# Head 0's queries in two token halves, ScalarE evicts the queries, and low parts behind a norm's first steps

## The reference, cut to what matters

```python
q = (zc @ peer_wq).reshape(128, 8, 2, 128)          # zc: 128 tokens, normalised
s1 = einsum('chd,hkd->chk', q[:, :, 0], k1)          # 128 keys per head and half
s2 = einsum('chd,hkd->chk', q[:, :, 1], k2)
v1, i1 = top_k(s1, 16); v2, i2 = top_k(s2, 16)
top_s, top_pos = top_k(v1[..., :, None] + v2[..., None, :], 16)   # of 256 candidates
gate = softmax(top_s)
act = gelu(einsum('chkd,cd->chk', peer_u[expert], zc))
out = einsum('chk,chkd->cd', gate * act, peer_v[expert])
```

## Time and profile before

| | us |
|---|---|
| median of three runs (2816.95 to 2819.15) | 2817.71 |
| the profiled execution, its own time | 2813.53 |
| its span in the profile | 2811.6 |
| TensorE busy | 2384.8 (85%) |
| VectorE busy | 1748.5 (62%) |
| ScalarE busy | 782.2 (28%) |
| GpSimd busy | 520.3 (19%) |

### The profile page before, as it was taken

One profiled execution on the slowest core, in us unless ns is written; L12 is line 12 of the kernel. 1 busy time (PEld: TensorE's weight loads), 2 busy tenths in 40 slices (PEclk: granted clock), 3 DMA queues, 4 the chain that ended last, 5 costly groups with the idle time before them and its releaser, 6 DMA issues.

```text
span 2811.6 us, 29260 instructions
## 1 busy us (share of the span) xinstructions
PE 2384.8 (85%) x10874; PEld 1692.4 (60%) x10874; DVE 1748.5 (62%) x2554; ACT 782.2 (28%) x1151; POOL 520.3 (19%) x594
## 2 busy tenths in 40 slices
PE   8998899999999999899899857777777777777776
PEld 8986677888888888799788722222222222222222
DVE  6975547665666566677656995555655555555444
ACT  5423555443444344545430101001010110111010
POOL 0000000000000000100012453333333333333341
PEclk9998899999999999999999989999999999999999
DMA  7643254556555655544588999999999999999997
GB/s 223 185 99 119 74 168 148 190 183 194 181 193 180 193 180 168 176 150 150 164 255 305 421 420 422 422 421 421 422 421 421 422 421 422 421 421 421 421 422 326
DMA packets 339901, 798.92 MB, mean 284 GB/s; under 512 B 23313, under 2 KB 270699, under 8 KB 273771
## 3 DMA queue, kind: packets, MB, share of 16 engines
q0 software_dynamic: 73728, 536.90, 45.9%
q1 hardware_dynamic: 266091, 260.96, 29.3%
HBM read 795.72 MB, written 2.10 MB: 284 GB/s over the span
## 4 chain that ended last, share of the span: by engine, by line
DMA 37%; PE 13%; DVE 7%; issue 1%; POOL 1%; ACT 1%; DVEq 0%; POOLq 0%; PEldq 0%; ACTq 0%
DMA row<-in_peer_v,expert 30%; DMA row<-in_peer_u,expert 6%; DVE row L2145 4%; PE pl L798 3%; PE pl L1143 3%; PE pl L805 3%; PE pl L1082 1%; PE pl L801 1%; PE pl L802 1%; POOL row L709 1%; DVE wlo L1649 1%; DMA raw<-in_w_out 0%; ACT whi L1170 0%; DVE sq_r L2165 0%; DVE l_xc L2031 0%
## 5 line engine op out<-in xcount | busy, mean ns | idle before, releaser
L1143 PE MATMUL pl<-row,diag 128*128 128x512 f32 x1856 | 860.1, 607 | 332.3 <-DMA row<-in_peer_v,expert 327.2
L2145 DVE CUSTOM_DVE_ANT_0 row<-row,pg 128x2048 f32<-128x2048 f32 x256 | 581.6, 2286 | 444.9 <-DMA row<-in_peer_u,expert 443.5
L1143 PEld LDWEIGHTS pl<-row,diag 128*128 128x128 f32 x1856 | 337.7, 191 | 854.7 <-issue 456.5
L1649 DVE TENSOR_TENSOR wlo<-raw,whi 128x1024 fp32r<-128x1024 f32 (+1 forms) x436 | 517.1, 1207 | 378.3 <-ACT whi L1170 375.9
L1170 ACT ACTIVATE whi<-raw 128x1024 fp32r<-128x1024 f32 (+1 forms) x436 | 443.6, 1039 | 420.9 <-PE pl L805 401.7
L798 PE MATMUL pl<-x_split,whi 128*128 128x512 f32 x1888 | 477.6, 395 | 13.0 <-DVE x_split L1657 7.5
L798 PEld LDWEIGHTS pl<-x_split,whi 128*128 128x128 f32 x1888 | 341.5, 190 | 76.5 <-issue 9.2
L805 PE MATMUL pl<-x_split,wlo 128*128 128x256 f32 x2656 | 373.2, 284 | 6.1 <-DVE wlo L1649 6.1
L805 PEld LDWEIGHTS pl<-x_split,wlo 128*128 128x128 f32 x2656 | 358.6, 192 | 25.7 <-DVE wlo L1649 7.1
L709 POOL DMA_INDIRECT row<-in_peer_u,expert x256 | 240.7, 940 | 634.9 <-PE pl L1143 500.0
L1562 ACT ACTIVATE diag<-ident,dots 128x128 f32<-128x128 f32 x232 | 90.8, 399 | 887.4 <-PE pl L1143 861.0
(11 more groups left out here) (312 smaller groups left out, 1545.9 us busy)
## 6 DMA issues: line engine op xcount, KB each, us to landing
raw<-in_w_in SPq DMA_DIRECT2D x50, 1024.0 KB, 5.4
raw<-in_w_gate SPq DMA_DIRECT2D x44, 1024.0 KB, 5.1
raw<-in_w_up SPq DMA_DIRECT2D x44, 1024.0 KB, 5.1
raw<-in_w_out SPq DMA_DIRECT2D x32, 1024.0 KB, 5.5
raw<-in_w_down SPq DMA_DIRECT2D x32, 1024.0 KB, 5.4
wq<-in_peer_wq SPq DMA_DIRECT2D x16, 1024.0 KB, 11.2
raw<-in_w_down SPq DMA_DIRECT2D x16, 768.0 KB, 4.6
raw<-in_w_ukv SPq DMA_DIRECT2D x4, 1024.0 KB, 5.1
```

What stands on the lines that cost most here:

```text
L1143: last = mm(pl[q], diag[:, (at - 1) % 4, :], row[b][:, q * 512:(q + 1) * 512], start=(t == 1 and n == 0 and k == 0), stop=last_row, skip_g ...
L1649: V.tensor_tensor(wlo[:, n % 4, 0:k, :], w[:, :, f, :], whi[:, n % 4, 0:k, :].bitcast(F32), ALU.subtract)\
L2145: V.tensor_tensor_reduce(row[b][:], row[b][:], z_tok[:], 1.0, 0.0, ALU.mult, ALU.add, dots[:, at:at + 1])\
```

## The change

- Head 0's queries are made for the first 128 tokens (matmuls of 128 columns), its scores for them follow, and the second 128 tokens come behind all token-row transposes. `wq_used` 1 comes with the latter.
- ScalarE copies the queries out of PSUM, unscaled (`query_copy`), and the exponent of the gate is taken with the token's norm factor as its scale. `EVICT` and VectorE's `queries` go.
- The first block's choice is split: expert numbers 0 to 7 are worked out and released (`sel_first`) ahead of the second pass of the maximum, and 8 to 15 behind it. In block 0, `best_keys` for block 1 moves from product 3 to 8, `choose` from 6 to 10.
- The two tiles of a head's weights from head 1 on share a semaphore, and both halves wait for both tiles.
- In `residual`, the low weights of half 0 move from ahead of the norm to pass 2, those of half 1 from pass 3 to pass 4.

```diff
-        wq_in = [sem(f"wq_in{m}") for m in range(2 * PH)]
+        wq_in = [sem(f"wq_in0{m}") for m in range(2)]
+        wq_in += [s for s in [sem(f"wq_in{n}") for n in range(1, PH)] for _ in range(2)]
...
-                if table == "u" and k == 0:
+                if j == 0:
+                    pool.wait_ge(sel_first, 1)
+                elif (table == "u" and k == 0) or j == 8:
                     pool.wait_ge(sel_ready, t * PH + n + 1)
...
-                    pe.wait_ge(wq_in[2 * n + half], 16)
+                    pe.wait_ge(wq_in[2 * n + half], 32 if n else 16)
...
-            queries(0, (0,))
+            queries(0, (0,), (0,), q0_done)
             wide_total("n2")
-            queries(0, (1,))
-            peer_scores(0)
+            queries(0, (1,), (0,), q0_done)
+            peer_scores(0, (0,))
...
+            token_rows(0)
+            token_rows(1)
+            queries(0, tokens=(1,))
             queries(1)
             pe.wait_ge(tok_r, 8)
+            peer_scores(0, (1,))
             peer_scores(1)
...
+            def query_copy(n, tokens=range(TT), done=wq_used, ready=wq_ready):
+                act.wait_ge(done, 1 if done is q0_done else n + 1)
+                if n >= 2:
+
+                    act.wait_ge(sc_done, n)
+                c = slice(tokens[0] * P, (tokens[-1] + 1) * P)
+                copy(qh[:, n % 2, :, c], pl[n % 2].rearrange("p (f s) -> p f s", f=2)[:, :, c]).then_inc(ready, 1)
...
-                activation(g, g, ACT.Exp).then_inc(sel_exp, 1)
+                activation(g, g, ACT.Exp, scale=small[:, 56 + t:57 + t]).then_inc(sel_exp, 1)
...
-            for n in range(1, PH):
-                score_copy(n)
+            query_copy(0, (1,))
+            query_copy(1)
+            score_copy(0, (1,))
+            score_copy(1)
+            query_copy(2)
+            for n in range(3, PH):
+                query_copy(n)
+                score_copy(n - 1)
+            score_copy(PH - 1)
             gate_exp(0, 0)
...
-                weights_lo(unit, piece, halves=(0,))
                 dve.wait_ge(gained, 8 * turn)
...
-                    if k == 3:
-                        weights_lo(unit, piece, halves=(1,))
+                    if k in (2, 4):
+                        weights_lo(unit, piece, halves=(k // 2 - 1,))
...
-            queries(0)
...
-            choose(0, 0)
+            link(V.max(ctop[:, 0:8], cand[:]))
+            V.max_index(cpos[:, 0:8], ctop[:, 0:8], cand[:])
+            link(V.match_replace(cand2[:], ctop[:, 0:8], cand[:], NEG))
+            experts(0, 8, [work[:, m, :].rearrange("p (k j) -> p k j", k=8) for m in range(2)], sel_first)
+            link(V.max(ctop[:, 8:16], cand2[:]))
+            link(V.max_index(cpos[:, 8:16], ctop[:, 8:16], cand2[:]))
+            V.tensor_tensor(gate[:, 0:TOPK], ctop[:], ctop[:, 0:1].broadcast_to([P, TOPK]), ALU.subtract).then_inc(sel_max, 1)
+            experts(8, 16, [work[:, m, :].rearrange("p (k j) -> p k j", k=8) for m in range(2)], sel_ready)
...
-                    if (i, k) in EVICT:
-                        queries(EVICT[i, k])
```

More of the change, by code:

```diff
@@ L1069, in _, with queries @@
             pe.wait_ge(z_scaled, 8)
-            def queries(n, halves=(0, 1)):
-                bank = pl[n % 2]
+            def queries(n, halves=(0, 1), tokens=range(TT), done=wq_used):
+                bank, cols, width = pl[n % 2], tokens[0] * P, len(tokens) * P
                 for half in halves:
-                    if half == 0:
+                    if half == 0 and tokens[0] == 0:
                         pe.wait_ge(wq_ready, n + 1)
                     w = wq[2 * n + half]
-                    pe.wait_ge(wq_in[2 * n + half], 16)
+                    pe.wait_ge(wq_in[2 * n + half], 32 if n else 16)
@@ L1079, in queries @@
                     for t in range(KU):
                         for f in range(2):
-                            first = half == 0 and t == 0 and f == 0
-                            last = mm(bank[:, f * S:(f + 1) * S], w[:, t, f, :], mix[:, half * KU + t, :], start=first,
+                            first = half == 0 and t == 0 and f == 0 and tokens[0] == 0
+                            last = mm(bank[:, f * S + cols:f * S + cols + width], w[:, t, f, :],
+                                      mix[:, half * KU + t, cols:cols + width], start=first,
@@ L1083, in queries, with peer_scores @@
                                       stop=(half == 1 and t == KU - 1), skip_group_check=True)
                     if half == 1:
-                        last.then_inc(wq_used, 1)
-            def peer_scores(n):
-                pe.wait_ge(wq_ready, n + 3)
+                        last.then_inc(done, 1)
+            def peer_scores(n, tokens=range(TT)):
+                if n == 0 and tokens[0] == 0:
+                    pe.wait_ge(q0_ready, 1)
+                else:
+                    pe.wait_ge(wq_ready, n + 3)
@@ L1090, in peer_scores @@
                 if n >= 2:
                     pe.wait_ge(sc_ready, 2 * (n - 1))
[L1093 to L1096, removed]
-                last.then_inc(sc_done, 1)
-            queries(0, (0,))
+                for t in tokens:
+                    for half in range(2):
+                        m = 2 * t + half
+                        last = mm(pl[2 + n % 2][:, m * P:(m + 1) * P], qh[:, n % 2, half, t * P:(t + 1) * P],
+                                  keysT[:, half * PH + n, :], start=True, stop=True)
@@ new lines, in peer_scores, with token_rows @@
+                last.then_inc(sc_done, 1)
+            def token_rows(t):
+                pe.wait_ge(norm_inv, NI["n2"] + 1)
+                for m in range(4 * t, 4 * t + 4):
+                    f4 = m % 4
+                    if m == 4:
+                        pe.wait_ge(rstd_tok, 1)
+                    elif m == 5:
+                        pe.wait_ge(sc_ready, 1)
+                    elif m >= 6:
+                        pe.wait_ge(tok_r, m - 1)
+                    bank = pg[f4] if t == 0 else pl[3 - m % 2]
+                    for f in range(4):
+                        last = nc.tensor.transpose(bank[:, f * P:(f + 1) * P],
+                                                   res[:, f4 * 4 + f, t * P:(t + 1) * P], ident[:])
+                    last.then_inc(tok_T, 1)
@@ L2156, in sum_row @@
                     .then_inc(row_summed, 1)
[L2158 to L2166, removed]
             def row_weights(pair):
@@ L2192, in final_rows, with experts @@
                         .then_inc(fin_out, 1)
-            queries(0)
-            best_keys(0, 0)
-            choose(0, 0)
+            def experts(n_first, n_last, halves, done):
+                m = slice(n_first, n_last)
+                ci = cpos[:, m].bitcast(I32)
+                V.tensor_scalar(cposi[:, 0, m], ci, 4, None, ALU.logical_shift_right)
+                link(V.tensor_scalar(cposi[:, 1, m], ci, 15, None, ALU.bitwise_and))
+                link(V.tensor_copy(cposf[:, :, m], cposi[:, :, m]))
+                full = [P, n_last - n_first, TOPK]
+                for half in range(2):
+                    last = V.tensor_tensor(halves[half], wide(cposf[:, half, m], 2, full),
+                                           iota16[:].unsqueeze(1).broadcast_to(full), ALU.is_equal)
+                link(last)
+                for half in range(2):
+                    last = V.tensor_tensor(halves[half], halves[half], wide(top_f[:, half, :], 1, full), ALU.mult)
+                link(last)
+                for half in range(2):
+                    last = V.tensor_reduce(cposf[:, half, m], halves[half], AX.X, ALU.add)
+                link(last)
+                V.scalar_tensor_tensor(expert[:, m], cposf[:, 0, m], float(NKEY), cposf[:, 1, m], ALU.mult, ALU.add).then_inc(done, 1)
+            best_keys(0, 0)
+            link(V.max(ctop[:, 0:8], cand[:]))
[6 more added lines that the diff above has]
+            experts(8, 16, [work[:, m, :].rearrange("p (k j) -> p k j", k=8) for m in range(2)], sel_ready)
+            dve.wait_ge(sel_ready, 1)
             dve.wait_ge(rstd_tok, 1)
```

31 lines of the change are left out of this document (10 added, 21 removed).

## The result

The kernel after took 2837.08 us (median of 4 runs, 2829.93 to 2841.28), the kernel before 2818.43 us beside it: a ratio of 1.0058, 95% interval 1.0037 to 1.008, slower by 18.7 us. Predicted were 2836 us and +18. The profiled execution of after is the lowest of its four: 2829.93 us, span 2827.8, granted clock 0.973; before's was 2813.53 us. The profiles are thus 16.4 us apart. In five further executions after had 2835.6 us and a ratio of 1.0059 (1.0046 to 1.0072).

What follows compares the result with a forecast made beforehand. The prediction took the gather phase, DMA at about 421 GB/s, as the bound, so idle DMA time decides. Head start -2.9, stall +20 and low parts +1.15 sum to +18: 2836 us, range 2815 to 2850.

Steps and rivals of the forecast that it cites:

- The gather start: Head 0's halves and the split choice: first gather at 1489.2 instead of 1498.13 us, 8.9 us earlier.
- 6.0 us of tiles pushed into the full stretch: Query-weight tiles 10 and 11, released at 1493.9 us, move inside the gathers and cost 6.0 us there.
- head start net -2.9: Gathers start 8.9 us earlier, less 6.0 us for tiles 10 and 11: 2.9 us gained.
- The share of 0.050 MB/us: DMA engines alternate gather and weight packets one for one, so a weight tile gets 0.050 MB/us, 21 us a tile.
- Dry time 2.7 us, last tile at 1606: Gather queue dry for 2.7 us behind the choice for block 1; last query-weight tile through at 1604, landed at 1606 us.
- Who waits: Head 7's queries wait for the last tiles, ScalarE and VectorE behind them; VectorE resumes 20.4 us after landing; DMA idle 20 us.
- ScalarE's evictions cost nothing: ScalarE's query copies, about 0.66 us per head, and the scale in the exponent add nothing on the path.
- Low parts: Low weights behind the norm in the residuals: 0.0 us in the first, +1.15 us in the second.
- The sum: Whole kernel: -2.9 + 20 + 1.15 = +18 us, giving 2836 us on the median of 2817.7.
- The tiles get through: Rival, chance 0.23: more dry time or a better share lands the last tile by 1592; -2 to +4 us, 2816 to 2822.
- Faster: Rival, chance 0.05: tiles fit into gaps of the gathers at 1495 to 1620 us; -8 us, 2810.

Runs made afterwards that it cites:

- run 12: The kernel after, unchanged, measured once more beside before: 2835.6 us, ratio 1.0059 to before.
- run 3: The kernel after with query-weight tiles 11, 13 and 15 issued on ScalarE's DMA queue instead of SyncE's: 2816.2 us, ratio 1.0001 to before.
- run 7: The kernel after with three tiles on ScalarE's DMA queue, exponents and first gelu ahead of head 7's query copy, low parts back: 2813.7 us, ratio 0.9988 to before.
- Run 8: The kernel after with head 0's queries for the second 128 tokens moved directly behind the first scores: 2813.1 us, ratio 0.9984 to before.
- run 11: The kernel after with query-weight tiles 10 to 15 each issued as two transfers, packets 0.5 KB instead of 1 KB: 2852.9 us, ratio 1.0122 to before.
- Run 5: The kernel after with ScalarE's first three exponents and first gelu put ahead of head 7's query copy: 2817.3 us, ratio 1.0006 to before.
- run 4: The kernel before with ScalarE's unscaled query evictions and the scale in the exponent, head 0 whole, low parts in the old place: 2817.0 us, ratio 0.9997.
- run 1: The kernel before with only the low parts moved behind the norm's first steps: 2819.1 us, ratio 1.0009.
- run 6: The kernel after with GpSimd waiting ahead of its row 24 until both tiles of head 7 have landed: 2821.6 us, ratio 1.0014 to before.
- run 2: The kernel after with the low parts back in their old place: 2831.2 us, ratio 1.0057 to before.

## Why the prediction was right, step by step

- **The gather start.** Forecast 1489.2, measured 1491.12; but the queries began 2.38 us later than in before. Relative to them, 9.4 us were gained for 8.9 (7.7 in run 12, the same kernel, where the first 5 us of the queries had a granted clock of 0.66). Records of 0.117 us for the assumed 0.125, and first scores selected at 1483.82 - 2.38 = 1481.4 for 1481.8: right.
- **6.0 us of tiles pushed into the full stretch**, head start net -2.9. Kernels without a stall measure it: run 3 lies 3.7 us under before in the table's last column, and so does run 7 less its slower first records; by its ratio, run 7 is 3.4 us under. Run 8, which moves part of these bytes back into the idle stretch, lies 5.5 under. Right, if a little small.
- **The share of 0.050 MB/us**: 0.81 MB in 16 us, as forecast, and shown by runs 3 and 11 to come from packets taken in turn. The Trainium skill's page "DMA: Bandwidth & Descriptors" (section Queues, rings and completion order) has each engine turn between queues at a whole packet, typically of 9 to 17 descriptors; the equal counts agree with turns. Were only the weights' packets that long, they would have had half of the bandwidth; they got 12% (0.81 of 6.60 MB). Were both sides' packets equally long, the bytes would divide as they did, so the trace doesn't speak against the page; how many pieces an engine takes at a turn, these counts don't tell.
- **Dry time 2.7 us, last tile at 1606.** It landed at 1605.8, but by two misses that cancel. By 1580 us 5.45 MB had moved (6.29 less 0.74 and 0.10), where the share alone gives 84.5 x 0.0504 = 4.26; the other 1.19 MB at 0.30 are **4.0 us of dry queue**, 1.3 more than taken, worth 7.7 us. Then the last 0.84 MB took until 1605.8, where the share gives 1596.7: a **tail of 9 us** that I had not in the sum. That the sum met 1606 is luck. The tail is not a lower share of all that was left. Queues of after from 1590 to 1594 us, then from 1596 to 1606:

```profile
q0 software_dynamic: 202, 1.46, 88.4%
q1 hardware_dynamic: 191, 0.19, 14.0%
...
q0 software_dynamic: 562, 4.08, 98.1%
q1 hardware_dynamic: 98, 0.10, 2.9%
```

  Until 1594 it is still nearly one for one, and by 1596 all but 0.10 MB were through, as the share says. The last 98 packets came spread over 10 us beside 562 of the gathers (65 beside 342 from 1600 to 1606 in run 12), and a tile has landed only with its last packet. That fits DMA engines which finish their parts of the tiles at different times; no view here shows a single engine, so the cause isn't shown.
- **Who waits.** Queries 15.5 us for 14.3 (a record took 0.243 us on average; the granted clock was 0.50 from 1600 to 1608, behind the wait of 22.6 us, and the first records ran at it). VectorE came to its wait at 1600.9, not at 1594, and resumed at 1625.7 for 1626.4. Idle 18.4 us for 20, with the second hole, 8 x (1 - 150/421.5) = 5.2 us from 1644 to 1652, for "about 5 near 1650". Run 5 shows that the late tile costs as much only through the chain over ScalarE and VectorE.
- **ScalarE's evictions cost nothing**: run 4, 0.9997. Right.
- **Low parts: mis-sized.** The two starts that it gave moved as forecast. First residual: ScalarE's root started at 418.62, where 421.75 less the 1.33 us by which after was then ahead is 420.42: 1.8 us earlier for 1.70. Second: the weight copy started at 1205.17, where 1202.49 plus the offset of 1.54 is 1204.03: +1.14 for +1.15. But the first residual was put at 0.0. From PE's first record of the norm's sum there (413.14 in before, 411.81 in after) to the one of the second residual (1180.14 and 1181.68) it is 767.0 us in before and 769.9 in after: **2.9 us** lost. All eight traces with the move have 769.9 (after, runs 1, 3, 5, 6, 8, 11, 12), all six without it 766.9 to 767.6. The sum had no term for TensorE's granted clock (last section).
- **The sum.** -2.9 + 20 + 1.15 = +18; by the medians +18.7. In the profiled pair: 13.8 from the queries on (1354.8 - 1341.0) for 17.1, and 2.4 ahead of them for 1.15. Those 2.4 are the 2.9 of the first residual and 0.8 behind the second, less 1.3 by which after was ahead before either. The stall was mis-sized by 1.6 us, the head start by about as much, and the low parts, in the profiles, by 2.6. The mechanism was right; that the total came out within 1 us owes something to misses that offset each other.
- **The rivals.** "The tiles get through" describes runs 3, 7 and 8, not after; its price, -2 to +4, is what runs 3 (+0.3 by the ratio) and 7 (-3.4, without the low parts' move) took, the latter roughly. "Faster" decides at 2.1 of the 6.0 us and not at 2.6 (-8.9 + 1.15 + 2.1 = -5.6).

## What to carry to other kernels

- When two DMA queues compete, count packets and not bytes: a load in 1 KB pieces beside gathers in 8 KB pieces gets an eighth. Moving half of it to a second queue was worth 16 us here, and releasing two of its tiles some 4 us earlier, before the gathers' packets, 21 us. A start that is made earlier takes an idle stretch away from whatever used to be loaded in it.
- Follow a late transfer through every in-order queue behind it: four calls moved ahead on ScalarE (run 5) hid nearly all of a 22 us wait that stayed where it was.

## What the runs showed that I had not expected

TensorE's granted clock fell after slightly longer waits in the residuals. Stretch 1215 to 1225 us, behind the second residual, in before, after, run 1 and run 2, in this order:

```profile
1215.00:1225.00 10.00, 10.00 (x73) 9.59 (x72) 4.94 (x15) 3.12 (x4) 0.00 (x0) 1.00 0.61 200
```

```profile
1215.00:1225.00 10.00, 10.00 (x55) 9.59 (x56) 3.58 (x5) 0.00 (x0) 0.00 (x0) 0.77 0.65 210
```

```profile
1215.00:1225.00 10.00, 8.15 (x44) 7.76 (x44) 5.57 (x37) 2.15 (x3) 0.00 (x0) 0.66 0.55 182
```

```profile
1215.00:1225.00 10.00, 10.00 (x73) 9.59 (x73) 5.40 (x19) 3.90 (x5) 0.00 (x0) 1.00 0.49 160
```

1.00 without the move of the low parts, 0.77 and 0.66 with it, and 1.00 again where it is undone: part of the stretch ran at 1.2 GHz, the lower of the two levels, and 55 matmul records got through instead of 73. Ahead of it PE had waited twice, here in after and then in before:

```profile
1212.14 0.39 PE L807 MATMUL pl<-x_split,whi 128*128 128x256 f32 x1 [2.01 <-DVE x_split L1877]
1214.72 2.08 PE L811 MATMUL pl<-x_split,wlo 128*128 128x256 f32 x8 [1.84 <-DVE wlo L1681]
```

```profile
1209.47 0.39 PE L801 MATMUL pl<-x_split,whi 128*128 128x256 f32 x1 [0.95 <-DVE x_split L1846]
1212.06 1.21 PE L805 MATMUL pl<-x_split,wlo 128*128 128x256 f32 x8 [1.84 <-DVE wlo L1649]
```

One wait of 2.01 instead of 0.95 us, and the next eight records take 2.08 us instead of 1.21. After fell from 1.5 to 4.8 us behind before at this place and had regained half of that by 1396 us, which is why the end saw little of it. The same happened behind the first residual (0.83 for 1.00 from 440 to 450 us), and once more at 1117 us, 670 us behind it, where both kernels wait equally long. Before, then after:

```profile
1117.06 1.65 PE L798 MATMUL pl<-h_split,whi 128*128 128x512 f32 x6 [2.03 <-ACT whi L1170]
1117.03 2.73 PE L804 MATMUL pl<-h_split,whi 128*128 128x512 f32 x6 [2.03 <-ACT whi L1186]
```

The six records behind it take 2.73 us instead of 1.65. Each of the two places costs about 1.5 us, and together they make up the 2.9 us. This is no accident of one trace: with the move, all eight traces show 0.83 in the 10 us from 27 us behind the first record of that norm's sum, and 2.73 to 2.83 us at the later place, and the six without it 1.00 and 1.64 to 1.65. So the length of the wait just ahead doesn't decide by itself; why the clock gives way at the later place only in kernels with the move stays open. In the first residual a wait of 1.76 us instead of 1.00 was thus followed by a loss of 1.5 us, more than the wait itself had grown.
